# Weighted sum over the index heads of the last key block on GpSimd, and top-k rounds ahead of the second attention

## The reference, cut to what matters

```
logits = einsum('bthd,bsd->bths', qi_blk, ki)             # 8 index heads
score = einsum('bths,bth->bts', relu(logits), wi_blk)     # weighted sum over the heads
score = where(key_pos <= t, score, -inf)
_, idx = lax.top_k(score, n_sel)                          # 128 of up to 512 keys
...                                                       # attention over the chosen keys
```

## Time and profile before

| | |
|---|---|
| Median of 3 runs | 1091.66 us (1089.81 to 1092.01) |
| Profiled execution, its own time | 1094.07 us |
| Its span, first to last instruction | 1092.3 us |
| Mean granted TensorE clock | 0.991 of full |
| TensorE / VectorE / ScalarE / GpSimd busy | 97% / 68% / 49% / 18% |
| HBM traffic | 91 GB/s over the span |

### The profile page before, as it was taken

The page is one execution under the profiler, slowest core; times in us unless marked ns, Lnnn a source line. Parts: engine busy times, 40 slices in busy tenths (PEclk is TensorE's granted clock), DMA queues, the critical chain, the costliest instruction groups (busy, mean ns, idle before and its releaser), DMA issues. The chain is left out here.

```text
span 1092.3 us, 14771 instructions
## 1 busy us (share of the span) xinstructions
PE 1057.5 (97%) x5372; PEld 858.4 (79%) x5372; DVE 743.5 (68%) x1282; ACT 540.3 (49%) x1012; POOL 193.4 (18%) x334
## 2 busy tenths in 40 slices
PE   7899999999999999999999888999999999999997
PEld 6677779988888888888778656679888888888885
DVE  4364644586697697687578788635586697696684
ACT  6477654454444444425554556655354453453421
POOL 1354520000000000005413367430000000000004
PEclk9999999999999999999999989999999999999999
DMA  9531505635355355332613324005635445545502
GB/s 294 115 78 39 117 1 116 136 78 116 79 115 116 83 111 116 87 68 53 142 30 83 72 53 103 1 1 116 136 79 115 100 94 116 103 90 116 107 9 78
DMA packets 52009, 99.94 MB, mean 91 GB/s; under 512 B 4704, under 2 KB 4832, under 8 KB 51936
## 3 DMA queue, kind: packets, MB, share of 16 engines
q1 hardware_dynamic: 51360, 98.87, 40.1%
q10 hardware_dynamic: 576, 0.11, 0.1%
HBM read 96.88 MB, written 2.10 MB: 91 GB/s over the span
## 5 line engine op out<-in xcount | busy, mean ns | idle before, releaser
L1947 PE MATMUL bank<-r_hi,w_hi 128*128 128x512 f32 (+1 forms) x456 | 177.7, 390 | 0.0
L1948 PE MATMUL bank<-r_hi,w_lo 128*128 128x512 f32 (+1 forms) x456 | 177.6, 389 | 0.0
L1949 PE MATMUL bank<-r_lo,w_hi 128*128 128x512 f32 (+1 forms) x456 | 177.6, 389 | 0.0
L1557 DVE TENSOR_TENSOR w_lo<-w_raw,w_hi 128x1024 fp32r<-128x1024 f32 x84 | 102.1, 1224 | 70.5 <-ACT w_hi L1099 70.4
L1099 ACT ACTIVATE w_hi<-w_raw 128x1024 fp32r<-128x1024 f32 x84 | 87.9, 1056 | 120.6 <-PE bank L1949 82.9
L2286 PE MATMUL bank<-w_hi,hid_hi 128*128 128x512 f32 x336 | 130.8, 389 | 0.0
L2288 PE MATMUL bank<-w_hi,hid_lo 128*128 128x512 f32 x336 | 130.8, 389 | 0.0
L2287 PE MATMUL bank<-w_lo,hid_hi 128*128 128x512 f32 x336 | 130.8, 389 | 0.0
L783 POOL TENSOR_TENSOR acc<-acc,G 128x512 f32<-128x512 f32 x8 | 13.0, 1652 | 594.3 <-ACT waste L963 594.3
L1108 ACT ACTIVATE w_hi<-w_raw,gT 128x512 fp32r<-128x512 f32 x96 | 64.5, 716 | 105.6 <-DMA w_raw<-in_w_mlp_up 74.2
L1949 PEld LDWEIGHTS bank<-r_lo,w_hi 128*128 128x128 f32 (+1 forms) x456 | 85.2, 187 | 18.3
(11 more groups left out here) (199 smaller groups left out, 2148.4 us busy)
## 6 DMA issues: line engine op xcount, KB each, us to landing
w_raw<-in_w_mlp_up SPq DMA_DIRECT2D x64, 512.0 KB, 6.5
w_raw<-in_w_mlp_down SPq DMA_DIRECT2D x64, 512.0 KB, 6.9
w_raw<-in_b_w_in SPq DMA_DIRECT2D x16, 512.0 KB, 6.8
w_raw<-in_a_w_in SPq DMA_DIRECT2D x8, 512.0 KB, 8.7
w_raw<-in_a_w_out SPq DMA_DIRECT2D x8, 512.0 KB, 5.9
w_raw<-in_b_w_out SPq DMA_DIRECT2D x8, 512.0 KB, 6.1
xt<-in_x_turned SPq DMA_DIRECT2D x8, 256.0 KB, 6.5
w_raw<-in_a_w_in SPq DMA_DIRECT2D x8, 256.0 KB, 6.7
```

The source lines that it names most:

```text
L1557: nc.vector.tensor_tensor(half_of(w_lo[:, u % 2, :], a), b_of(PRODUCTS[i][1], a), half_of(w_hi[:, u % 2, :], a).bitcast(f32), ALU.subtract ...
L1947: nc.tensor.matmul(bank, whi, xhi, start=start, stop=False)
L1948: nc.tensor.matmul(bank, wlo, xhi, start=False, stop=False)
L1949: return nc.tensor.matmul(bank, whi, xlo, start=False, stop=stop)
```

## The change: what it does

Heads of the last key block (X from 16 to 23, LAST_HEADS is 16) are weighted and summed on GpSimd (`accumulate_last`): for head 0 one product into `score`, for the others a product in place in the ReLU's buffer and an addition to `score`. The ReLU's buffers for this block are four in place of two, and ScalarE waits only for the head four before. GpSimd's queue takes four heads after the rotation of key block 1, two after that of block 2 and two after that of block 3. On VectorE the eight sums go, `causal(3)` moves behind block 1's top-k, and block 2 gets 13 rounds ahead of the attention (7 before); both tables change.

```diff
+LAST_HEADS = 2 * IDX_HEADS
+
+
+def relu_place(X):
+    return X % 2 if X < LAST_HEADS else X % 4
@@
-        relu = at("relu", [2, SEQ], f32, pt_at + 12288)
+        relu = at("relu", [4, SEQ], f32, pt_at + 8192)
@@ gpsimd
+            def accumulate_last(X_):
+                h = X_ - LAST_HEADS
+                v, r = score[:, NB - 2, :], relu[:, relu_place(X_), :]
+                weight = wi[:, NB - 1, h:h + 1].to_broadcast([P, SEQ])
+                pool.wait_ge(idx_relu, X_ + 1)
+                if h == 0:
+                    pool.wait_ge(wi_done, 1)
+                    nc.gpsimd.tensor_tensor(v, r, weight, ALU.mult).then_inc(last_acc, 1)
+                else:
+                    nc.gpsimd.tensor_tensor(r, r, weight, ALU.mult).then_inc(last_weighed, 1)
+                    pool.wait_ge(last_weighed, h)
+                    pool.wait_ge(last_acc, h)
+                    nc.gpsimd.tensor_tensor(v, v, r, ALU.add).then_inc(last_acc, 1)
@@
-                    for j in range(NB):
-                        rope_k(1, j)
+                    rope_k(1, 0)
+                    rope_k(1, 1)
+                    for X_ in range(LAST_HEADS, LAST_HEADS + 4):
+                        accumulate_last(X_)
+                    rope_k(1, 2)
+                    for X_ in range(LAST_HEADS + 4, LAST_HEADS + 6):
+                        accumulate_last(X_)
+                    rope_k(1, 3)
+                    for X_ in range(LAST_HEADS + 6, LAST_HEADS + 8):
+                        accumulate_last(X_)
@@ scalar, relued
-                if X_ >= 2:
-                    act.wait_ge(idx_acc, X_ - 1)
+                if X_ >= LAST_HEADS + 4:
+                    act.wait_ge(last_acc, X_ - LAST_HEADS - 3)
+                elif X_ >= 2:
+                    act.wait_ge(idx_acc, min(X_ - 1, LAST_HEADS))
@@ vector
-            for X_ in range(16, 20, 2):
-                accumulate(X_)
-                accumulate(X_ + 1)
+            for _ in range(3):
                 top_round([1])
             k_low(1, 1)
+            for _ in range(2):
+                top_round([1])
             split(56)
-            for X_ in range(20, 24, 2):
-                accumulate(X_)
-                accumulate(X_ + 1)
+            for _ in range(5):
                 top_round([1])
-            causal(3)
             split(57)
             k_low(1, 2)
             k_low(1, 3)
             top_rounds(1, TOPK // 8)
             top_mask(1)
+            causal(3)
+            top_rounds(2, 4)
             q_low(1, 11)
-            top_rounds(2, 1)
+            top_rounds(2, 7)
             split(58)
             q_low(1, 12)
-            top_rounds(2, 3)
+            top_rounds(2, 9)
             split(59)
             q_low(1, 13)
-            top_rounds(2, 5)
+            top_rounds(2, 11)
             q_low(1, 14)
-            top_rounds(2, 7)
+            top_rounds(2, 13)
-            ROUNDS_2 = (8, 9, 10, 12, 13, 14, TOPK // 8)
-            ROUNDS_3 = (0, 1, 2, 3, 4, 5, 6, 8, 10, 12, 14, TOPK // 8)
+            ROUNDS_2 = (14, 15, TOPK // 8)
+            ROUNDS_3 = (0, 1, 2, 4, 5, 7, 8, 10, 12, 14, 15, TOPK // 8)
```

More of the change, by code:

```diff
@@ L356, in hybrid_trunk @@
         idx_ready, idx_relu, idx_acc, top_v = sem("idx_ready"), sem("idx_relu"), sem("idx_acc"), sem("top_v")
+        last_weighed, last_acc = sem("last_weighed"), sem("last_acc")
         s_ready, s_masked, sink_put, exp_done = sem("s_ready"), sem("s_masked"), sem("sink_put"), sem("exp_done")
@@ L998, in relued @@
                 act.wait_ge(idx_ready, X_ + 1)
-                if X_ >= 2:
-                    act.wait_ge(idx_acc, X_ - 1)
-                nc.scalar.activation(relu[:, X_ % 2, 0:W], banks[idx_bank(X_)][:, 0:W], ACT.Relu).then_inc(idx_relu, 1)
+                if X_ >= LAST_HEADS + 4:
+                    act.wait_ge(last_acc, X_ - LAST_HEADS - 3)
+                elif X_ >= 2:
+                    act.wait_ge(idx_acc, min(X_ - 1, LAST_HEADS))
+                nc.scalar.activation(relu[:, relu_place(X_), 0:W], banks[idx_bank(X_)][:, 0:W], ACT.Relu).then_inc(idx_relu, 1)
             def expo(layer, n, c):
@@ L1284, in _ @@
             q_scaled(1, 2, 1)
-            act.wait_ge(idx_acc, 24)
+            act.wait_ge(last_acc, IDX_HEADS)
             attention(1)
@@ L1522, in accumulate @@
                 if h == 0:
-                    nc.vector.tensor_scalar(v, relu[:, X_ % 2, 0:W], wi[:, b, h:h + 1], None, ALU.mult).then_inc(idx_acc, 1)
+                    nc.vector.tensor_scalar(v, relu[:, relu_place(X_), 0:W], wi[:, b, h:h + 1], None, ALU.mult).then_inc(idx_acc, 1)
                 else:
@@ L1528, in causal @@
             def causal(b):
-                dve.wait_ge(idx_acc, 8 * b)
+                if b < NB - 1:
+                    dve.wait_ge(idx_acc, 8 * b)
+                else:
+                    dve.wait_ge(last_acc, IDX_HEADS)
                 v = score[:, b - 1, b * P:(b + 1) * P]
```

## The result

Before 1091.66 us (median of 11 runs, 1089.81 to 1094.73), after 1095.01 us (11 runs, 1093.24 to 1098.52). The ratio is 1.0031, 95% interval 1.0019 to 1.0042: slower by 3.4 us. The forecast was 1092.5 (0.8 us slower), inside 1088.2 to 1096.0; of its cases it is "slower by the clock" that came.

The account below looks back on a forecast made before the run. TensorE's own queue was taken to set the end, other engines counting only where it waits. Terms of +1.9 and -1.1 us gave +0.8, so 1092.5 us for the median, range 1088.2 to 1096.0.

Parts of the forecast that it names:

- slower by the clock: Rival: TensorE's wait at about 580.5 to 582.3 us brings half clock, +2.5 and up to +4 us; chance 0.23.
- term 2: Second attention: earlier masks shorten TensorE's waits near 637 and 661 us, partly replaced by waits for GpSimd; -1.1 us.
- Heads on GpSimd: Ahead of the second attention: a product takes 1.04 us, an addition 1.26, a later head 2.3.
- the upper bound: Ahead of the second attention: every GpSimd operation at 1.35 us, a head 2.7, product at 584.5; +3.7 us.
- Term 1: Ahead of the second attention: GpSimd's heads delay the last key rotation and split 57, so TensorE waits; +1.9 us.
- The clock I leave at a net of nothing: Half-clock stretch at 638 to 642 us may go, a new one may come behind the wait near 580; net 0.
- there the wait moves from VectorE to GpSimd: Second attention, transposes at 670.81 us: GpSimd's probabilities become the limit, so no more than 1.1 us of the gain survives.
- The extra mask of block 2: Second attention, ahead of turn 4's masks: the final mask comes one turn earlier, 0.5 us, leaving 0.5 us net gain.
- Each of the six added rounds would cost its 1.25 us: VectorE ahead of the second attention: added rounds cost nothing under ScalarE's cover, 1.25 us each if it were gone.

Follow-up runs that it names:

- The later split: ScalarE's split of unit 63 moved from turn 6 to turn 7, an edit put on several kernels; on rotation first the attention went from 113.6 to 110.5 us.
- rotation first: Changed kernel with GpSimd's rotation of key block 3 moved ahead of heads 20 and 21; ratio to the kernel before 1.0069.
- quiet 57: Rotation first, with GpSimd adding heads 20 to 23 only after VectorE's split of unit 57, now after 3 rounds; 60.2 us ahead of the attention, 111.8 inside.
- 63 later: Here the kernel before with only ScalarE's split of unit 63 moved from turn 6 to turn 7; ratio 1.0020, attention 113.8 us against 113.6.

## Why the prediction was right or wrong

- What bounds the kernel: right. TensorE's queue sets the end: the part behind the attention had the same length, 362.2 or 362.3 us, in all kernels, and the part ahead of it 54.4 to 54.6 us in the three where TensorE has no new wait there.
- The time lies in the range, which is 7.8 us wide; the forecast itself had 0.8 of the 3.4 us. Two of its steps were wrong, the clock and the end of term 2, both to the same side. "Slower by the clock" was priced at +2.5 with term 2's -1.1 in it; without that it would have been +3.6.
- Heads on GpSimd: sizes right, 1.04 and 1.28 us where 1.04 and 1.26 were taken. The 1.35 us an operation of the upper bound came only beside splits.
- Term 1, +1.9 us: right in place, mechanism and size. TensorE waited 2.06 us for the rotation of block 3 behind two heads, and the product that stood at 580.82 came 1.8 us later. Split 56, beside head 19 and the rotation of block 2, took 4.27 us (4.4 forecast). Split 57, forecast at 579.6 in the time of the kernel before, which is 576.1 here, started at 575.54; it was not held up by head 5's addition but itself slowed, 3.04 us.
- "The clock I leave at a net of nothing": this step failed. Behind the wait the clock was 0.90 and 0.68 in two stretches of 4 us where it had been 1.00, and nine products took 1.5 us more. The text had said that the clock would decide where the wait reaches about 2 us, priced it at 1.7, and gave it 0.23. All eight kernels with a wait of over 2 us ahead of the attention (2.06 to 4.80) had such a fall behind it, and their stretch is 1.2 to 1.8 us longer than its waits explain; this should have been part of term 1. Inside the attention the same does not hold (below), and there the text's doubt was in place.
- Term 2, -1.1 us: the wait at 637.64 shrank to 0.56, the one at 661.53 and the stretch at 638 went, better than forecast (3.3 us by 660). Then it was given back. The step that failed is "there the wait moves from VectorE to GpSimd": GpSimd's chain did come 1.9 us earlier (665.06 for 666.97), but TensorE's next wait was for masks, 1.98 us, that hung on ScalarE's place for unit 63. Net 0.1 instead of 1.1. The later split shows it, 3.1 us in rotation first and 1.6 in quiet 57. The half-clock stretches sum to the same: 638 went, 668 came, and luck has a part in where they fall.
- The extra mask of block 2 a turn earlier took 0.36 us (0.5 was taken). The wait for masks at 627.56 is 1.84 where it was 1.19, but with the tables of before it is 1.65 in three other runs: 0.2 us of it is the table's, the rest is that TensorE had been at 0.59 just there in the kernel before.
- "Each of the six added rounds would cost its 1.25 us" if the cover were gone: the run with 13 rounds and all heads on VectorE came to that. Six rounds more ahead of split 58 are 7.5 us; VectorE had stood idle there for 0.96 and 2.98 us, and TensorE waited for the rest, 3.64 us.
- Clashes of a VectorE instruction with two SBUF operands and GpSimd: the Trainium skill, SBUF — State Buffer, Who interferes with whom, has the direction right. By mutual exclusion of whole instructions a split (0.69 alone) and a GpSimd addition (1.28) or product (1.04) would take 1.97 or 1.73 us a pair; measured, four splits beside heads throughout took 6.26, 1.57 each, and the head's operations 1.48 and 1.59 each. So each is slowed, but less than the rule says, as the row of the kernel before had it.

What stays open: why the kernel before with the later split alone measured 1.0020 with no longer stretch in its trace, what decides in the attention whether the clock falls, and whether a better table of rounds would keep both 54.4 and 110.4 us.

## What to carry to other kernels

Before work goes to an idle engine, add up its time in the window in which it must be done, not over the span, and see what runs beside it: GpSimd was busy for 18% of the span, but from its first head to the first query ready for it there are 20.6 us for 19.5 us of work at the best, and beside VectorE's splits both engines slow down. Where a wait of TensorE of 2 us or more is created, price it as the wait and the half-clock stretch that may follow. And where a gain inside a stage disappears, look for the next queue that holds an instruction waiting for a transfer ahead of work that is ready: two edits that are each worth nothing gave about 3 us together (113.6 us to 110.5, 110.2 and 111.0).

## What the runs showed of the hardware

- The slowing of VectorE and GpSimd by each other depends on the VectorE instruction. Four splits of 512 columns: 2.74 us alone, 3.04 beside rotations, 4.27 beside a head and a rotation, 6.26 beside heads throughout. Weighted sums of a score row: 1.61 for two alone, 3.39 for four beside rotations. MAX8 and MATCH_REPLACE8 kept 0.97 to 0.99 us a round of 256 columns beside the heads, and the heads kept 1.04 and 1.28 to 1.31.
- A rotation's small GpSimd operation (128x32) is 0.25 us alone and 0.70 beside a VectorE split or weighted sum; a product of 512 columns goes from 1.04 to 1.48. By share the small ones suffer most (2.8 times, against 2.3 for the splits and 1.4 for the product).
- A GpSimd operation with a broadcast column as second operand takes 1.04 us for 512 columns, with two full operands 1.28.
- The length of a wait does not decide by itself whether TensorE's clock falls behind it, once TensorE is busy again. Waits of 2.06 to 4.80 us ahead of the attention always had a half-clock stretch for a part of the following 4 to 8 us, one of 1.75 us (quiet 57, 586.59) had none. In the attention the same wait came out either way: 1.98 us for masks was followed by 0.58 in the changed kernel and by 0.80 and 0.77 in rotation first, 1.99 us in quiet 57 by 1.00; the one of 1.72 us at 661 in the kernel before by 1.00, the same one, 1.71 us, at 658.78 in the kernel before with 63 later by 0.63 in 660 to 664.
- The products of 512 columns start every 0.23 us at the full clock and every 0.43 us in the half-clock stretch (579 to 582.5 in the changed kernel).
